# The output gates of eight heads as four pairs of seven half products, in a hybrid decoder layer

## The reference

```python
o_r = jax.nn.silu(r_z) * head_norm(ret, ret_gn_g).astype(dt)
...
o_m = jax.nn.silu(m_z) * head_norm(hm, ml_gn_g).astype(dt)
```

## Time and profile before

| what | value |
|---|---|
| median of 3 runs | 1479.52 us |
| the profiled execution's own time | 1478.4 us |
| its span, first to last instruction | 1476.6 us |
| PE busy, 10318 matmuls | 1458.7 us (99%) |
| DVE, ACT, POOL busy | 914.5, 520.1, 580.5 us |
| matmuls of units (L1155 to L1157) | 3 x 960 |
| matmuls of windows (L1204 to L1206) | 3 x 1568 |
| HBM read, written | 110.99, 35.64 MB |

### The profile page before, as it was taken

One profiled execution on the slowest core, in us unless ns is written; L12 is line 12 of the kernel. 1 busy time (PEld: TensorE's weight loads), 2 busy tenths in 40 slices (PEclk: granted clock), 3 DMA queues, 4 the chain that ended last, 5 costly groups with the idle time before them and its releaser, 6 DMA issues.

```text
span 1476.6 us, 26706 instructions
## 1 busy us (share of the span) xinstructions
PE 1458.7 (99%) x10318; PEld 1420.6 (96%) x10318; DVE 914.5 (62%) x1786; ACT 520.1 (35%) x1071; POOL 580.5 (39%) x456
## 2 busy tenths in 40 slices
PE   8999999999999999999999999999999999999998
PEld 8999999999999999999999999999999999999786
DVE  6455352556666665677977878867656324885542
ACT  6342333333334345333333342334454422220221
POOL 1000000000011021787777767776777844662100
PEclk9999999999999999999999999999999999999999
DMA  8120222212021121322223221222222476754222
GB/s 316 44 87 29 89 67 80 74 44 91 30 91 62 58 80 50 106 92 91 67 94 95 87 81 68 73 102 88 95 81 102 148 238 207 234 159 149 109 83 78
DMA packets 65527, 148.37 MB, mean 100 GB/s; under 512 B 7976, under 2 KB 36920, under 8 KB 65272
## 3 DMA queue, kind: packets, MB, share of 16 engines
q1 hardware_dynamic: 58008, 120.06, 24.3%
q0 software_dynamic: 6192, 22.27, 4.2%
q10 hardware_dynamic: 1200, 4.33, 0.7%
HBM read 110.99 MB, written 35.64 MB: 99 GB/s over the span
## 4 chain that ended last, share of the span: by engine, by line
PE 88%; DVE 5%; DMA 2%; POOL 2%; issue 1%; ACT 1%; SPq 0%; DVEq 0%; ACTq 0%; POOLq 0%
PE bank L1204 11%; PE bank L1206 11%; PE bank L1205 11%; PE bank L1155 9%; PE bank L1157 9%; PE bank L1156 9%; PE bank L1222 4%; PE bank L1223 4%; PE bank L1224 4%; PE bank L1416 1%; PE bank L1417 1%; PE bank L1418 1%; PE sums_ps L1312 1%; PE sums_ps L1327 1%; PE sums_ps L1331 1%
## 5 line engine op out<-in xcount | busy, mean ns | idle before, releaser
L1155 PE MATMUL bank<-h_hi,w_hi 128*128 128x352 f32 x960 | 319.4, 333 | 1.2 <-POOL w_lo L1802 1.0
L1157 PE MATMUL bank<-h_hi,w_lo 128*128 128x352 f32 x960 | 309.2, 322 | 0.0
L1156 PE MATMUL bank<-h_lo,w_hi 128*128 128x352 f32 x960 | 308.4, 321 | 0.0
L1204 PE MATMUL bank<-h_hi,t_hi 128*128 128x264 f32 x896 | 256.2, 286 | 0.0
L1205 PE MATMUL bank<-h_lo,t_hi 128*128 128x264 f32 x896 | 254.6, 284 | 0.0
L1206 PE MATMUL bank<-h_hi,t_lo 128*128 128x264 f32 x896 | 254.1, 284 | 0.0
L1802 POOL TENSOR_TENSOR t_lo<-stage,t_hi 128x512 fp32r<-128x512 f32 x144 | 194.7, 1355 | 139.5 <-ACT t_hi L1458 139.4
L1204 PE MATMUL bank<-c_hi,t_hi 128*128 128x264 f32 x672 | 191.3, 285 | 2.1 <-DVE part L2073 2.1
L1206 PE MATMUL bank<-c_hi,t_lo 128*128 128x264 f32 x672 | 191.0, 284 | 0.0
L1205 PE MATMUL bank<-c_lo,t_hi 128*128 128x264 f32 x672 | 190.3, 283 | 0.0
L1155 PEld LDWEIGHTS bank<-h_hi,w_hi 128*128 128x128 f32 x960 | 180.5, 188 | 2.9 <-POOL w_lo L1802 1.3
(11 more groups left out here) (369 smaller groups left out, 2879.2 us busy)
## 6 DMA issues: line engine op xcount, KB each, us to landing
stage<-in_wa SPq DMA_DIRECT2D x64, 512.0 KB, 3.3
piece<-g_rows SPq DMA_DIRECT2D x96, 176.0 KB, 2.7
stage<-in_wg SPq DMA_DIRECT2D x32, 512.0 KB, 3.5
g_rows<-sgt SPq DMA_DIRECT2D x120, 132.0 KB, 1.9
o_raw<-o_rows SPq DMA_DIRECT2D x16, 528.0 KB, 6.2
stage<-in_wb SPq DMA_DIRECT2D x32, 256.0 KB, 2.8
xt<-in_xT SPq DMA_DIRECT2D x6, 704.0 KB, 12.7
o_rows<-zs POOLq DMA_DIRECT2D x8, 528.0 KB, 3.0
```

The source lines that it names most:

```text
L1155: pe.matmul(out, hi, h_hi[:, k, tok(b)], start=(k == 0), stop=False)
L1156: pe.matmul(out, hi, h_lo[:, k, tok(b)], start=False, stop=False)
L1157: mm = pe.matmul(out, lo, h_hi[:, k, tok(b)], start=False, stop=(k == KD - 1))
L1204: pe.matmul(out, hi, a_hi(k), start=(first and k == 0), stop=False, skip_group_check=True)
```

## The change

The z units leave the stages: head 0's stage has 30 slots, mlstm(1) to mlstm(3) 24 each, the retention stages 18 and the last one 24. The tasks get new places in them. `pt` now multiplies by the gain alone, and the normed outputs go to `o_rows` ungated. Four windows of a new kind zz, one for two heads, compute both z tiles; SP loads the two heads' outputs from `o_rows` into cc[2] and cc[3] (`zload`), DVE multiplies them as in cz, and POOL stores them back (`zspill`). There are 32 windows instead of 28, and the LayerNorm's places move by 44 slots. The six first tiles of the first window are split behind the last two units (four and two) instead of the last three (two each).

```diff
 IFC, IFW = 8, 40
 ORDER = (1, 3, 0, 2)
 PLAIN_GATES = 2
-LN_AT = ((254, 260, 261, 264, 268, 269, 271), (274, 280, 281, 284, 288, 289, 299), (303, 309, 310, 313, 317, 318, 321))
+LN_AT = ((298, 304, 305, 308, 312, 313, 315), (318, 324, 325, 328, 332, 333, 343), (347, 353, 354, 357, 361, 362, 365))
...
         return [("rq", cols(2048, h), h + 4), ("rk", cols(2560, h), h + 4), ("rv", cols(3072, h), h + 4)]
 
     def z(hd):
-        return [("z", cols(7680, hd) if hd < 4 else cols(3584, hd - 4), hd)]
-
-    def late(group, late_unit):
-
-        return group[:2] + late_unit + group[2:]
+        return cols(7680, hd) if hd < 4 else cols(3584, hd - 4)
 
     gate_units = [n * KD + j for n in ORDER for j in range(KD)]
 
...
     for c in range(0, CH, 2):
         gates[32 + c // 2] = [("mw", c), ("mw", c + 1)]
     gates[35].append(("mws",))
-    phase([("if", ("wi", 0), 0)] + mlstm(0)[:2] + z(0) + mlstm(0)[2:], gates)
+    phase([("if", ("wi", 0), 0)] + mlstm(0), {x: step for x, step in gates.items() if x < 30})
     for h in range(1, 4):
         if h == 1:
-            phase(mlstm(1), {x: step for x, step in zip((1, 3, 5, 6, 8, 9, 11, 12, 14, 15, 16, 17, 19, 21, 22), attention(0))})
+            tasks = {x - 30: step for x, step in gates.items() if x >= 30}
+            for x, step in zip((7, 8, 9, 10, 11, 12, 13, 14, 15, 16, 18, 19, 20, 22, 23), attention(0)):
+                tasks.setdefault(x, []).extend(step)
+            phase(mlstm(1), tasks)
         else:
-            phase(late(mlstm(h), z(h - 1)), spread(attention(h - 1), 0, 2.05))
+            phase(mlstm(h), spread(attention(h - 1), 0, 1.62))
     for h in range(4):
 
-        steps = attention(h + 3)
-        tasks = spread(steps[:6], 0, 2)
-        for x, step in zip((12, 13, 14, 15, 17, 18, 19, 22, 23), steps[6:]):
+        tasks = {}
+        for x, step in zip((0, 1, 2, 3, 4, 6, 7, 8, 9, 10, 12, 13, 14, 16, 17), attention(h + 3)):
             tasks.setdefault(x, []).extend(step)
         if h:
-            for i, x in enumerate((16, 18, 19, 20, 20, 21)):
+            for i, x in enumerate((13, 14, 15, 15, 16, 17)):
                 tasks.setdefault(x, []).append(("comb", h - 1, i))
             for c in range(3):
-                tasks.setdefault((22, 23, 23)[c], []).append(("comb_split", h - 1, c))
-        phase(late(ret(h), z(h + 3)), tasks)
+                tasks.setdefault(17, []).append(("comb_split", h - 1, c))
+        phase(ret(h), tasks)
 
     tasks = {}
-    for x, step in zip((0, 1, 2, 4, 5, 6, 8, 9, 11, 13, 15, 16, 17, 18, 19), attention(7)):
+    for x, step in zip((0, 1, 2, 4, 5, 6, 8, 9, 10, 12, 13, 15, 16, 18, 20), attention(7)):
         tasks.setdefault(x, []).extend(step)
     for i in range(6):
         tasks.setdefault(2 * i + 1, []).append(("comb", 3, i))
     for c in range(3):
         tasks.setdefault(14 + 2 * c, []).append(("comb_split", 3, c))
     for k in range(4):
-        tasks.setdefault((20, 22, 24, 26)[k], []).append(("comb4", k))
+        tasks.setdefault(20 + k, []).append(("comb4", k))
     glu0 = [("cv", cols(4096, 0), 0), ("cg", cols(4608, 0), 0)]
-    phase(late(glu0, z(7)) + [("g", ("wg", n), n) for n in gate_units[:PLAIN_GATES]], tasks)
+    phase(glu0 + [("g", ("wg", n), n) for n in gate_units[:PLAIN_GATES]], tasks)
...
     def out_c(g):
         return ("cz", g, (cols(5120, g), cols(5120, g + 1)))
 
-    late_tasks = {0: [("hist", 1), ("ahist",)], 1: [("t4", k) for k in range(4)]}
+    def out_heads(q):
+        return ("zz", q, (z(2 * q), z(2 * q + 1)))
+
+    late_tasks = {0: [("hist", 1), ("ahist",)], 1: [("t4", k) for k in range(4)], 9: [("zload", 0)]}
 
     def tasks_at(at, *steps):
         late_tasks.setdefault(at, []).extend(steps)
 
     room = []
-    for what in (None, glu(1), None, conv_a(0), None, out_a(0), None, glu(2), None, conv_a(1), None, glu(3), None, out_a(1),
-                 conv_a(2), None, out_a(2), None, conv_a(3), None, out_a(3), None, None, None, out_c(0), out_c(2),
-                 None, None):
+    for what in (None, out_heads(0), glu(1), out_heads(1), None, out_heads(2), conv_a(0), out_heads(3), None, glu(2), None,
+                 out_a(0), None, conv_a(1), None, glu(3), None, out_a(1), conv_a(2), None, out_a(2), None, conv_a(3), None,
+                 out_a(3), None, None, None, out_c(0), out_c(2), None, None):
         kind = what or gate_pair()
         at = 14 * len(pairs)
         if kind[0] == "cvcg":
             tasks_at(at + 16, ("ext_out", kind[1]))
         if kind[0] == "abaz":
             tasks_at(at + 16, ("spill", 8 + kind[1]))
+        if kind[0] == "zz":
+            tasks_at(at + 16, ("zspill", kind[1]))
+            if kind[1] < 3:
+                tasks_at(at + 22, ("zload", kind[1] + 1))
...
-        free = {"cvcg": (0, 1, 2, 5, 6, 9, 10), "acau": (0, 1, 2, 5, 6, 9, 10), "abaz": (0, 1, 2, 5, 6)}.get(
+        free = {"cvcg": (0, 1, 2, 5, 6, 9, 10), "acau": (0, 1, 2, 5, 6, 9, 10), "abaz": (0, 1, 2, 5, 6), "zz": (0, 1, 2, 5, 6)}.get(
...
         for place_, step in zip(LN_AT[b], ("ln0", "lnm", "ln1", "ln1b", "lnv", "lns", "ln2")):
             tasks_at(place_, (step, b))
     for g in range(4):
-        tasks_at(324 + 4 * g, ("ln3a", g))
-        tasks_at(326 + 4 * g, ("ln3", g))
-    assert at <= LN_AT[0][0] and 338 <= 14 * 24 + 8, at
+        tasks_at(368 + 4 * g, ("ln3a", g))
+        tasks_at(370 + 4 * g, ("ln3", g))
+    assert at <= LN_AT[0][0] and 382 <= 14 * 28 + 8, at
...
         if u and u + RING < n1:
             emit_split(("plain", u + RING))
             lows.append(at_split[("plain", u + RING)])
-        if u >= n1 - 3:
-            for i in range(2 * (u - n1 + 3), 2 * (u - n1 + 4)):
+        if u >= n1 - 2:
+            for i in range((0, 4)[u - n1 + 2], (4, 6)[u - n1 + 2]):
                 emit_split(("win", 0, i))
 
 
...
                     sp.wait_ge(piece_used, x - (6 if x < 48 else 5) + 1)
                 sp.dma_start(piece[piece_slot(x)][:, :], g_rows[unit, :, tok(b)]).then_inc(piece_in[piece_slot(x)], 16)
 
-            walk({"load": load, "blk": blk, "prod": prod, "oload": oload, "gload": gload})
+            def zload(q):
+
+                if q == 0:
+                    sp.wait_ge(o_out, 16 * 8)
+                    sp.wait_ge(t4_lo, 4)
+                else:
+                    sp.wait_ge(z_out, 32 * q)
+                for i in range(2):
+                    sp.dma_start(cc[2 + i][:, :], o_rows[out_row(2 * q + i)]).then_inc(z_in, 16)
+
+            walk({"load": load, "blk": blk, "prod": prod, "zload": zload, "oload": oload, "gload": gload})
 
...
-                elif kind == "z":
-                    if b == 0 and 3 <= info < 7:
-
-                        act.wait_ge(qkv_dve, info + 2)
-                    sigmoid_to_sg(u, b, ps)
                 elif kind == "cv":
                     act.activation(cb[:, tok(b)], ps, ACT.Copy).then_inc(freed["A"], 1)
                 elif kind == "cg":
+                    if b == 0:
+
+                        act.wait_ge(qkv_dve, 8)
                     sigmoid_to_sg(u, b, ps)
                     act.wait_ge(sg_ready, SGN[(u, b)] + 1)
...
+            def zspill(q):
+
+                pool.wait_ge(z_gated, 2 * q + 2)
+                for i in range(2):
+                    pool.dma_start(o_rows[out_row(2 * q + i)], cc[2 + i][:, :]).then_inc(z_out, 16)
+
...
-                elif kind == "z":
-                    hd, m = info, SGN[(u, b)]
-                    dve.wait_ge(sg_ready, m + 1)
-                    if b == 0 and hd:
-
-                        dve.wait_ge(o_out, 16 * hd)
-                    TT(zs[:, tok(b)], ps, sg[m % 2][:, :], ALU.mult).then_inc(sg_used, 1)
-                    dve.wait_ge(sg_used, m + 1)
-                    dve.sem_inc(freed["V"], 1)
...
-                elif i == P2 and kind == "cz":
+                elif i == P2 and kind in ("cz", "zz"):
+                    second = gated_tiles(w)[1]
                     g22 = sgt_of((w, 22, tp))
                     dve.wait_ge(r22_done, n)
+                    if kind == "zz" and not tp:
+                        dve.wait_ge(z_in, 32 * (info + 1))
                     own(TT(u3, u3, g22[:, :], ALU.mult))
                     own.wait()
-                    own(TT(cc[info + 1][:, odd], u3, cc[info + 1][:, odd], ALU.mult))
+                    own(TT(second[:, odd], u3, second[:, odd], ALU.mult))
                     own.wait()
                     dve.sem_inc(eaten, 1)
                     if tp:

...
             def pt(hd, half):
                 gain = vc[:, hd % 4, (V_MG if hd < 4 else V_RG):(V_MG if hd < 4 else V_RG) + 1]
                 parts = [(tb, slice(0, 512)), (pb, slice(512, 1024))] if half == 0 else [(tb, slice(TP, T))]
+                if half == 0 and hd:
+                    dve.wait_ge(o_out, 16 * hd)
                 for i, (t, s) in enumerate(parts):
                     dve.wait_ge(pt_ready, 3 * hd + 1 + i + 2 * half)
                     w_ = s.stop - s.start
```

(10 more changed lines are left out.)

39 lines of the change are left out of this document (21 added, 18 removed).

## The result

The changed kernel takes 1510.02 us (median of 4 runs, 1508.39 to 1510.69), the kernel before 1479.19 us in the same session (1478.79 to 1479.61): a ratio of 1.0205, 95% interval 1.0193 to 1.0218. It is slower by 30.8 us. The forecast was 1501, its own range 1487 to 1513. Its mean granted clock was 0.995, that of the others 0.992 or 0.993.

A forecast was written before the change was run, and what follows sets the result against it. TensorE's own work was taken to bound the kernel. From 1478.4 us: -9.96 arithmetic, -2.1 head 7's transpose, +22.7 over the heads, +8.5 start of pairs, +1.5 clock, +1.0 pairs = 1500.0; plus 1.1 for the median, 1501, range 1487 to 1513.

The forecast's parts named there:

- (g): The pairs themselves: loads and stores cost nothing, banks come free late in the fourth zz pair; 1.0 us, bounds 0 and 6.
- head 7's last transpose: End of head 7: the transpose gets two slots instead of one, which takes its wait away; 2.1 us returned.
- (a): Retention stages: rotation on DVE delays the next slot's attention step, 7.3 us, and the samples' vx, 1.0; bounds 0 and 12.
- (b): Heads 0 to 3: a sigmoid table load makes the second attention step late, 4.0 us; bounds 3 and 5.
- (c): Norm before the output transposes: 3.6 us late for head 3, about 0.35 each for heads 4 to 6; bounds 2 and 7.
- (d): Combinations around the output transposes: first gain product late, 2.1 us, next head's kw late, 3.6; bounds 1 and 9.
- (e): Start of the pairs: comb4 starts late behind POOL's queue, so u2 is late; 8.5 us, bounds 2.3 and 11.9.
- (f): Clock at the start of the pairs: the long wait lowers it to 0.50; 1.5 us, bounds 0 and 4.
- Rival 3: Clock stays low for 12 us of work at the pairs or in the heads: 1509 us, chance 0.08.
- Rival 1: Covers hold in the stages, DVE and ACT catch up within each slot: faster, 1467.5 us, chance 0.12.
- Rival 2: Only the heads wait; POOL splits early and comb4 runs at 0.71 per operation: 1493 us, chance 0.15.
- Rival 4: About half of all predicted waits come: 1480 to 1484 us, chance 0.06.

The follow-up runs named there:

- e2: Changed kernel with the rotary embedding's addition done at the next block's first slot, behind the attention step: 1501.23 us, ratio 1.0145.
- e3: Changed kernel with a one-column sigmoid on ACT at the first attention step of heads 0 to 3, before kw: 1506.54 us, ratio 1.0187.
- e4: Changed kernel with the norm's second half one slot earlier, on DVE ahead of the rotation and low weight part: 1505.34 us, ratio 1.0171.
- e5: Changed kernel with a row's last two combinations and three comb_split moved to slot 5 of the next stage: 1513.44 us, ratio 1.0226.
- e7: Changed kernel with POOL's sums and low parts of the first pair's weights replaced by memsets, leaving those out of the computation: 1499.61 us, one run.
- c2: Changed kernel with repairs to rotation, table load, norm, combinations and pairs together, and comb4 in halves through PSUM: 1474.80 us, ratio 0.9972.
- b1: The kernel before with only the rotation's addition behind the attention step and comb4 in halves through PSUM: 1480.61 us, ratio 1.0010.
- e6: Changed kernel with comb4's last rows and the taps behind u2, comb_split earlier, LayerNorm 12 slots later: 1503.72 us, ratio 1.0167.

## Why the prediction was right, step by step

The sign, the place of nearly every wait and the arithmetic came out; the sum was 9 us short. Waits are the gaps less 0.16, and (g) is read from the lengths of the pairs.

| step | predicted | measured |
|---|---|---|
| four pairs for eight units | -9.96 | -9.96 less what stands at (g) |
| head 7's last transpose | -2.1 | -2.0 (gap 2.21 to 0.25) |
| (a) rotation ahead of a step; vx | 7.3; 1.0 | 8.2; 1.1 |
| (b) table load | 4.0 | 4.0 (4 x 0.99) |
| (c) norm: head 3; heads 4 to 6; head 0 | 3.6; 1.05; 0 | 3.6; 1.4; 1.8 |
| (d) gain product; kw | 2.1; 3.6 | 1.1; 3.0 |
| (e) start of the pairs | 8.5 | 11.7 |
| (f) clock | 1.5 | 2.1 |
| (g) pairs | 1.0 | 3.5: 1.1 around the fourth, 2.4 at the LayerNorm |

The right column adds up to 29.5 of the 30.0 us by which the span grew; 0.5 more stand at head 0's first step (its gap went from 1.58 to 2.03), which other traces show at 1.71 to 2.49. The forecast added 1.1 us for the median over the profiled execution; the changed kernel's median is 1.6 above its own.

(a) was right to 0.1 at eight of the twelve places: six gaps of 0.77 to 0.79 are waits of 0.62, two of head 3's are 0.52, and e2 took them away by moving just the addition. Larger were the three at slots 1 to 2 (gaps of 1.36, 1.16, 1.15), which the prediction priced at 0.63; e2 removed them too. Smaller was head 3's at the same slots, 0.25. Of vx, heads 4 to 6 bring 1.1; head 3's gap of 0.43 stood in the kernel before as 0.46.

(b) was exact, and e3 takes the waits away by the step that the prediction named, the table load between kw and so.

(c) was exact for head 3, by the sum of what stands between the two halves of the norm, and e4 confirms the order as the cause. For heads 4 to 6 the recorded 0.35 does not follow from its own numbers (3.64 less 2.87 less 0.7 is 0.07); they measured 0.40 to 0.57. The step that failed is "Steps of mLSTM stages in adjacent slots cost nothing else". Head 0's norm costs 1.8. Its stage keeps its 24 slots, but the second half of the norm now stands three slots behind the statistics instead of two, and so behind the low weight part (1.22 us), which came after it before; and TensorE wants the output 0.64 us sooner after the samples' step (14.38 instead of 15.02). e4 puts the low part back behind the norm, and the gap goes from 1.93 to 0.80.

(d) was counted too high for the gain product (0.36 each instead of 0.7) and somewhat too high for kw (1.0 instead of 1.2). e5 shows that the same work is late in another slot too, where a step of ACT stands behind it.

(e) is the term mis-sized. The chain is the predicted one: GpSimd began its nine operations 2.7 us after slot 17 (2.8 predicted), comb_split ended 1.5 after the pair began (1.8), comb4 started at once and took 15.3 us (14), and so ended at 559.14, 16.8 after the pair's start (15.8). Then 5.0 us of t4, tap 0, two taps and u2 follow, and TensorE resumes 21.8 after the pair's start, where its work alone gives 8.8. By its own chain the prediction had 15.8 less 5.0, that is 10.8 more than before, and took 8.5 between its ends 2.3 and 11.9; the discount had no row behind it, and the wait grew by 11.7. The growth itself is the late start: comb4 began 9.9 us ahead of the first pair and now begins 1.5 behind it, and takes 15 us both times. That it stays at 15 instead of 8.5 is the reason the prediction gave for its upper end, the Trainium skill's rule (GPSIMD Engine Reference, section 8 Key points) on two SBUF inputs, and e7 and c2 agree with it.

(f): the low level lasted 4.5 us into the work, not 3. Rival 3, a long stay at the low level, did not come. The sentence that the 1.88 us idle at 591.90 did not lower the clock holds for that trace; in b1's the clock fell for 3.4 us, from 593.16, behind the same wait.

(g): the LayerNorm's places were moved by 44 slots while the branch C gate pairs moved by 56. The prediction read the shift and not what it stood beside. Around the fourth zz pair it named the cause, tap_a; c2, where a pair g stands in its place, has no wait there. e6 gave the 12 slots back and 1.8 us of waits with them.

Rival 1 (covers hold) needed waits under 12 us in (a) to (d); they are 24. Rival 2 had 11.5 us too little at the pairs, 2.3 where (e) and (f) came to 13.8. Rival 4 (about half of all waits) did not come either. With the upper value of (e) the forecast would have been 1504. The other misses partly cancel: (c) and (g) were 2.1 and 2.5 short, (d) 1.6 too high.

## What to carry to other kernels

Work taken out of a stage takes away its cover too: the change gained 10 us and uncovered 41, nearly all of it found by asking of each step what stands ahead of it in its engine's queue. Most of it was order and came back by moving small things (one addition, one dummy sigmoid, one task by a slot), and only with these is the cheaper arithmetic faster. Where VectorE and GpSimd work at the same time on the critical path, let VectorE's operations read one operand from PSUM. It costs ScalarE a copy into it.
